# Hybrid decoder step: the last fixed expert pair added to the tokens by weighted slot matmuls

## The reference

```python
w_top = softmax(top_v) * p_sel                       # two weights per token
act = silu(hf @ w_eg[e]) * (hf @ w_eu[e])            # each expert: 1024 -> 256
out = out + (act * combine[:, e]) @ w_ed[e]          # 256 -> 1024
x = x + out
y = x * rsqrt(mean(x * x) + EPS) * norm_final
```

## Time and profile before

| | |
|---|---|
| Median of 3 runs | 797.81 us (797.54 to 798.9) |
| Profiled execution | 798.78 us, its span 796.7 us |
| Granted TensorE clock, mean | 0.979 |
| TensorE matmul, busy | 715.7 us, 90% |
| VectorE, ScalarE, GpSimd busy | 340.8, 246.0, 82.2 us |
| DMA | 172.49 MB, mean 216 GB/s |
| Chain that ended last | PE 69%, SP's queue 14%, DVE 8%, DMA 4%, ACT 3% |

### The profile page before, as it was taken

One profiled execution on the slowest core, in us unless ns is written; L12 is line 12 of the kernel. 1 busy time (PEld: TensorE's weight loads), 2 busy tenths in 40 slices (PEclk: granted clock), 3 DMA queues, 4 the chain that ended last, 5 costly groups with the idle time before them and its releaser, 6 DMA issues.

```text
span 796.7 us, 12378 instructions
## 1 busy us (share of the span) xinstructions
PE 715.7 (90%) x5118; PEld 534.2 (67%) x5118; DVE 340.8 (43%) x630; ACT 246.0 (31%) x496; POOL 82.2 (10%) x135
## 2 busy tenths in 40 slices
PE   4999999999999999999999999989999977777730
PEld 3888997778999999778999977864444422222210
DVE  6653359654565336435344532751323211111128
ACT  6233474544454342334222232411111100100013
POOL 2404000000000100000000010221113121111100
PEclk9999999999999999999999999989999999999985
DMA  8732111113132722613223289889999999999945
GB/s 314 230 107 62 54 53 53 54 53 106 54 98 62 264 82 99 220 53 97 62 80 110 78 297 398 302 284 374 419 415 418 418 418 417 419 419 419 412 163 219
DMA packets 82503, 172.49 MB, mean 216 GB/s; under 512 B 8064, under 2 KB 42208, under 8 KB 82432
## 3 DMA queue, kind: packets, MB, share of 16 engines
q1 hardware_dynamic: 72736, 148.51, 50.2%
q0 software_dynamic: 9712, 23.20, 7.9%
HBM read 162.73 MB, written 18.74 MB: 228 GB/s over the span
## 4 chain that ended last, share of the span: by engine, by line
PE 69%; SPq 14%; DVE 8%; DMA 4%; ACT 3%; issue 2%; POOLq 0%; ACTq 0%; DVEq 0%
PE bank L756 44%; SPq L566 10%; PE bank L1219 7%; PE bank L1235 4%; SPq L572 3%; DMA expert_down<-in_w_exp_down 2%; DVE w_split L1593 2%; PE bank L1151 1%; ACT w_split L1273 1%; PE bank L776 1%; PE bank L1186 1%; PE bank L1041 1%; PE bank L1047 1%; DMA x_rows<-in_x_prompt 1%; DVE token_out L2185 1%
## 5 line engine op out<-in xcount | busy, mean ns | idle before, releaser
L756 PE MATMUL bank<-hT_split,w_split 128*128 128x272 f32 x1152 | 154.1, 292 | 0.0
L756 PEld LDWEIGHTS bank<-hT_split,w_split 128*128 128x128 f32 x1152 | 147.4, 188 | 2.1 <-issue 0.9
L1219 PE MATMUL bank<-expert_gate_up,gatheredT 128*64 128x512 f32 x512 | 115.0, 595 | 21.3 <-DMA expert_gate_up<-in_w_exp_up 20.4
L756 PE MATMUL bank<-w_split,hT_split 128*128 128x512 f32 (+1 forms) x576 | 130.9, 381 | 0.4 <-DVE w_split L1593 0.4
L756 PEld LDWEIGHTS bank<-w_split,hT_split 128*128 128x128 f32 x576 | 100.6, 189 | 23.1 <-issue 3.3
L1593 DVE TENSOR_TENSOR w_split<-w_raw,w_split 128x2048 fp32r<-128x2048 f32 (+1 forms) x35 | 75.9, 2168 | 83.7 <-ACT w_split L1273 83.7
L1219 PEld LDWEIGHTS bank<-expert_gate_up,gatheredT 128*64 128x64 f32 x512 | 39.4, 137 | 93.7 <-issue 62.8
L1273 ACT ACTIVATE w_split<-w_raw 128x2048 fp32r<-128x2048 f32 (+1 forms) x35 | 63.4, 1812 | 42.4 <-PE bank L756 17.5
L1235 PE MATMUL bank<-expert_down,expert_actT 128*64 128x512 f32 x256 | 58.5, 597 | 13.2 <-DMA expert_down<-in_w_exp_down 8.1
L2156 DVE TENSOR_TENSOR expert_act<-expert_silu,bank 128x256 f32<-128x256 f32 x16 | 6.7, 421 | 119.5 <-ACT expert_silu L1547 119.5
L756 PE MATMUL bank<-gla_outT_split,w_split 128*128 128x272 f32 x384 | 49.4, 288 | 0.0
(11 more groups left out here) (372 smaller groups left out, 837.0 us busy)
## 6 DMA issues: line engine op xcount, KB each, us to landing
expert_gate_up<-in_w_exp_gate SPq DMA_DIRECT2D x64, 512.0 KB, 14.4
expert_gate_up<-in_w_exp_up SPq DMA_DIRECT2D x64, 512.0 KB, 15.3
expert_down<-in_w_exp_down SPq DMA_DIRECT2D x32, 1024.0 KB, 17.2
w_raw<-in_w_in SPq DMA_DIRECT2D x15, 1024.0 KB, 5.5
w_raw<-in_w_in SPq DMA_DIRECT2D x16, 512.0 KB, 4.7
s_state<-in_state_gla POOLq DMA_DIRECT2D x4, 1024.0 KB, 9.5
out_sample_gla_state<-s_state POOLq DMA_DIRECT2D x4, 1024.0 KB, 6.1
w_raw<-in_w_proj_gla SPq DMA_DIRECT2D x8, 512.0 KB, 4.4
```

What stands on the lines that cost most here:

```text
L756: ins = mm(out, stat(x, k), mov(y, k), start=first and n == 0 and m == 0, stop=last and n == len(ks) - 1 and m == 2)
L1219: ins = mm(P[2 + u][64 * half:64 * half + 64, :].rearrange("p (m n) -> p m n", m=2), XT[0][:, k, 64 * half:64 * half + 64], WGU[gb][:, k / ...
```

## The change

- Pair 15 (the last fixed pair, now always done last, outside the loop) isn't scattered. Its result stays in `YO`. A one-hot matrix, slot by token, carries each slot's weight (`SPREAD_LAST`), and a matmul adds the pair to the tokens in PSUM. The slots' weights come from ten small matmuls behind pair 1 (three bf16 digits).
- For blocks 0 to 2 the second expert's rows are added in PSUM too, by a matmul with a diagonal of `w2`. For the sampled block one matmul (`ST4`) makes `x + w1 * y1 + w2 * y2`.
- Rows of `tok_d` that pair 15 would have written must be zero, so GpSimd stores zeros to all 1088 rows in nine chunks, each behind one unit from 22 to 30.
- The rows are read back behind pair 14's scatter, to a weight buffer that pair 13 used last.
- The row `norm_final` is spread behind the tenth pair, and `keep_clock(5)` becomes `keep_clock(6)`.
- Two pairs are done after the loop (14 and 15), the loop does pairs 12 and 13 and any overflow, and the overflow pieces shift.

```diff
-PEELED = NFIX // 2 - 1
+PEELED = NFIX // 2 - 2
+SEQ = NFIX - 2
+ZERO_CHUNKS = -(-2 * NTOK // 128)
+BY_PE = (0, 1, 2)
...
+    YI = [at(f"token_out_{n}", [128, D], F, D0 + 49152 + 4096 * n) for n in range(2 * NB - 2)]
...
-            sp.wait_ge(scattered[0], 16 * turns)
-            sp.wait_ge(scattered[1], 16 * turns)
+            for kh in range(2):
+                sp.wait_ge(gu_done, 2 * (SEQ - 3) + kh + 1)
+                load_gate_up(2, pair(SEQ), kh)
+            sp.wait_ge(dn_done, SEQ - 2)
+            load_down(2, pair(SEQ))
...
+            sp.wait_ge(scattered[0], 16 * turns + 16)
             for bl in range(NB):
                 for k in range(2):
-                    sp.dma_start(YI[2 * bl + k][0:rows(bl), :],
-                                 tok_d[k * NTOK + bl * 128:k * NTOK + bl * 128 + rows(bl), :]).then_inc(x_in[bl], 16)
+                    dst = YI[2 * bl + k][:] if bl < 4 else X2[32 + 32 * k:64 + 32 * k, 4, :]
+                    sp.dma_start(dst, tok_d[k * NTOK + bl * 128:k * NTOK + bl * 128 + rows(bl), :]).then_inc(x_in[bl], 16)
...
+            pool.memset(ZEROS[:], 0.0).then_inc(pool_wrote, 1)
+            pool.wait_ge(pool_wrote, 1)
+            for c in range(ZERO_CHUNKS):
+                pool.wait_ge(main_mm, unit_done(OUT_UNIT - ZERO_CHUNKS + c))
+                n = min(128, 2 * NTOK - 128 * c)
+                pool.dma_start(tok_d[128 * c:128 * c + n, :].rearrange("p (c n) -> p c n", n=256),
+                               ZEROS[0:n, :].unsqueeze(1).to_broadcast([n, 4, 256])).then_inc(zeros_stored, 16)
...
-            pool.dma_start(NFIN[0:1, :], a["norm_final"].unsqueeze(0)).then_inc(nfin_in, 16)
...
+            pool.wait_ge(zeros_stored, 16 * ZERO_CHUNKS)
             for i in range(PEELED):
                 for u in range(2):
                     move_rows(i, u)
+                    if 2 * i + u == 2:
+                        pool.dma_start(NFIN[0:1, :], a["norm_final"].unsqueeze(0)).then_inc(nfin_in, 16)
+                        pool.wait_ge(slots_hot, 5)
+                        for k in range(2):
+                            pool.dma_start(W4[32 + 32 * k:64 + 32 * k, :], R1[f"w{k + 1}"][0:32, 4:5]).then_inc(w4_in, 16)
...
+            move_rows(turns, 0, last=True)
...
-            pe.wait_ge(nfin_in, 16)
-            for c in range(2):
-                ins = mm(P[2 + c][:], ONEROW[:], NFIN[0:1, 512 * c:512 * c + 512], start=True, stop=True)
-            ins.then_inc(nfin_mm, 1)
-            keep_clock(5)
+            keep_clock(6)
...
-                pe.wait_ge(gathered[v], 16 * i + (16 if u == 0 else 32))
-                turn_rows(v)
+                if not (last and u):
+                    pe.wait_ge(gathered[v], 16 * i + (16 if u == 0 else 32))
+                    turn_rows(v)
...
+                    if 2 * i + u == 1:
+                        pe.wait_ge(slots_hot, 5)
+                        slot_table(P[5][:, 320:323], OHR, LASTD, range(2 * NB)).then_inc(table_mm, 1)
...
+                    if 2 * i + u == 9:
+                        pe.wait_ge(memset_done, 2)
+                        pe.wait_ge(nfin_in, 16)
+                        for c in range(2):
+                            ins = mm(P[2 + c][:], ONEROW[:], NFIN[0:1, 512 * c:512 * c + 512], start=True, stop=True)
+                        ins.then_inc(nfin_mm, 1)
+                        pe.wait_ge(nfin_out, 1)
...
+            for u in range(2):
+                expert_pair(turns, u, last=True)
+
+            pe.wait_ge(spread_ready, 1)
+            for bl in range(NB):
+                cols = slice(128 * bl, 128 * bl + rows(bl))
+                banks = [P[2 * (bl % 4) + c][0:rows(bl), :] for c in range(2)]
+                if bl == 4:
+                    pe.wait_ge(x3_ready, 1)
+                if bl in BY_PE or bl == 4:
+                    pe.wait_ge(x_in[bl], 16 + 32)
+                    for c in range(2):
+                        half = slice(512 * c, 512 * c + 512)
+                        if bl == 4:
+                            mm(banks[c], ST4[0:96, :], X2[0:96, 4, half], start=True, stop=False)
+                        else:
+                            mm(banks[c], DIAG2[bl][:], YI[2 * bl + 1][:, half], start=True, stop=False)
+                if bl == 0:
+                    pe.wait_ge(y_out_a, 2 * turns + 3)
+                    pe.wait_ge(y_out_v, 2 * turns + 3)
+                for c in range(2):
+                    ins = mm(banks[c], SPREAD_LAST[:, cols], YO[:, 512 * c:512 * c + 512], start=bl not in BY_PE and bl < 4, stop=True)
+                ins.then_inc(sums_mm, 1)
...
+                    if j == 0:
+                        act.wait_ge(zeros_stored, 16 * ZERO_CHUNKS)
...
+                    if 2 * i + u == 9:
+                        act.wait_ge(nfin_mm, 1)
+                        A(NFIN[:, 0:512], P[2][:], ACT.Copy)
+                        A(NFIN[:, 512:D], P[3][:], ACT.Copy).then_inc(nfin_out, 1)
...
+                if bl < 4:
+                    act.wait_ge(x3_ready, bl + 1)
+                else:
+                    act.wait_ge(sums_mm, NB)
...
-            V.memset(ONEROW[:], 1.0)
...
+            V.tensor_tensor(SLOT[:, 0:1], IF1[:, NFIX - 1:NFIX], P[6][:, 2 * NFIX - 1:2 * NFIX], ALU.add)
...
+            for k in range(2):
+                js = slice(NB * k, NB * k + NB)
+                link(V.tensor_tensor(LASTW[:, js], R1[f"w{k + 1}"][:], PAIRH[:, js, NFIX - 1], ALU.mult))
...
+            V.tensor_copy(LASTD[:, :, 2, 0], LASTR[:]).then_inc(slots_hot, 1)
+
+            def last_weights():
+                dve.wait_ge(table_mm, 3)
+                V.tensor_reduce(SLOT[:, 1:2], P[5][:, 320:323], axis=AX.X, op=ALU.add)
+                V.memset(W4[0:32, :], 1.0)
+                V.memset(ONEROW[:], 1.0).then_inc(memset_done, 1)
...
-            OVER_PARTS = {1: over_tiles, 2: over_ranks, 3: over_places, 4: over_onehots, 5: over_experts, 6: over_turns, 9: over_rows}
+            OVER_PARTS = {3: last_weights, 1: over_tiles, 2: over_ranks, 4: over_places, 5: over_onehots, 6: over_experts, 7: over_turns, 9: over_rows}
...
+                if last and u:
+                    first_expert(0)
+                else:
+                    dve.wait_ge(xg_turned, n + 3)
+                    xt_half()
...
+            link(V.memset(IONES[:], 1.0))
+            link(V.tensor_tensor_scan(out=IOTA[:], data0=IONES[:], data1=IONES[:], initial=-1.0, op0=ALU.mult, op1=ALU.add))
+            V.scalar_tensor_tensor(out=SPREAD_LAST[:], in0=IOTA[:], scalar=SLOT[:, 0:1], in1=SLOT[:, 1:2].to_broadcast([128, NTOK]),
+                                   op0=ALU.is_equal, op1=ALU.mult)
+            for bl in BY_PE:
+                V.scalar_tensor_tensor(out=DIAG2[bl][:], in0=ident, scalar=R1["w2"][:, bl:bl + 1], in1=ident, op0=ALU.mult, op1=ALU.mult)
+            same = cst("same_head")
+            dve.wait_ge(w4_in, 32)
+            for p0, p1, q in ((0, 64, 0), (64, 96, 64)):
+                ins = V.scalar_tensor_tensor(out=ST4[p0:p1, :], in0=same[p0:p1, q:q + 32], scalar=W4[p0:p1, :],
+                                             in1=same[p0:p1, q:q + 32], op0=ALU.mult, op1=ALU.mult)
+            ins.then_inc(spread_ready, 1)
+            added = {}
+
+            def first_expert(bl):
+                y1 = YI[2 * bl][:]
                 dve.wait_ge(x_in[bl], 16 + 32)
-                link(V.scalar_tensor_tensor(out=y1[0:n, :], in0=y1[0:n, :], scalar=R1["w1"][0:n, bl:bl + 1], in1=X2[0:n, bl, :],
-                                            op0=ALU.mult, op1=ALU.add))
-                V.scalar_tensor_tensor(out=y1[0:n, :], in0=y2[0:n, :], scalar=R1["w2"][0:n, bl:bl + 1], in1=y1[0:n, :],
-                                       op0=ALU.mult, op1=ALU.add).then_inc(x3_ready, 1)
+                chain[0] += 1
+                added[bl] = chain[0]
+                V.scalar_tensor_tensor(out=y1, in0=y1, scalar=R1["w1"][:, bl:bl + 1], in1=X2[:, bl, :],
+                                       op0=ALU.mult, op1=ALU.add).then_inc(dve_step, 1)
+
+            def second_expert(bl):
+                y1 = YI[2 * bl][:]
+                dve.wait_ge(dve_step, added[bl])
+                chain[0] += 1
+                added[bl] = chain[0]
+                V.scalar_tensor_tensor(out=y1, in0=YI[2 * bl + 1][:], scalar=R1["w2"][:, bl:bl + 1], in1=y1,
+                                       op0=ALU.mult, op1=ALU.add).then_inc(dve_step, 1)
+
+            def banks_sum(bl):
+                y1 = two_halves(YI[2 * bl][:])
+                dve.wait_ge(dve_step, added[bl])
+                dve.wait_ge(sums_mm, bl + 1)
+                V.tensor_tensor(y1, BANKS[:, 2 * bl:2 * bl + 2, :], y1, ALU.add).then_inc(x3_ready, 1)
 
...
-            for bl in range(NB + 1):
-                if bl < NB:
-                    add_experts(bl)
-                if bl:
-                    last_norm(bl - 1)
+                x3, y = (YI[2 * bl][:], YI[2 * bl][:]) if bl < 4 else (None, OUT4[0:n, :])
```

(46 more changed lines are left out.)

83 lines of the change are left out of this document (55 added, 28 removed).

## The result

The changed kernel takes 788.74 us (median of 4 runs, 785.64 to 790.65) against 797.67 (797.09 to 798.90) for the kernel before on the same chip. The ratio is 0.9882, with a 95% interval of 0.9848 to 0.9916. The profiled execution has a span of 786.6 us, 10.1 less than before.

What follows compares the result with a forecast made beforehand. Matmuls were taken to bound the kernel up to about 535 us, then the stream of expert weights, then the tail. Span 796.7 - 9.1 - 0.5 = 787.1; time 788.2 us off the median, own range 787.0 to 789.5.

Steps and rivals of the forecast that it cites:

- Part 1: Tail: scatter and reads leave the path, first rows at 763.9; delay taken as 0, other bound 3.3 us.
- Part 2: Tail on TensorE: nine pairs of new-sum matmuls at 1.73 us, 15.6 us, ending at 780.6.
- Part 3: Tail on VectorE: 16.6 us of work, ending at 785.2 instead of 794.36; the tail gives back 9.1 us.
- Part 4: Before pair 0: norm matmuls leave, a sixth clock-keeping matmul comes; start up to 1.1 us earlier, 0.5 us saved.
- rival 1: Pair 0 meets the half clock: up to 6.0 us, 3.5 for half of its first half; chance 0.13.
- Part 5: Work costed at nothing: zeros in the projection units, slot weights, norm's 3 us stop behind pair 9, other small moves.
- Rival 2: Tail: reads delay the last weights (3.3 us, 791.5) or VectorE's half of the copy (2.2 us, 790.4); chance 0.12.
- Rival 3: Tail: the final sums run at half clock and the kernel is slower, 802.2 us; chance 0.04.

Runs made afterwards that it cites:

- late_reads: Changed kernel, with SP also waiting for pair 15's down matmuls before it reads the tokens back; 796.19 us, 0.9980 of the kernel before.
- block0_dve: Changed kernel, with TensorE making the second products of blocks 1, 2 and 3 instead of 0, 1 and 2, VectorE block 0's; 786.98 us, 0.9864.
- seconds_dve: Changed kernel, with the second products of blocks 0, 1 and 2 moved from TensorE to VectorE; 788.54 us, 0.9888.
- norm_back: Changed kernel, with the norm row spread ahead of pair 0 again, five clock-keeping matmuls and no stop behind pair 9; 788.72 us, 0.9877.
- zeros_three: Changed kernel, with each chunk of zeros stored three times, to the scratch and two spare ones nobody reads; 789.35 us, 0.9895.
- hold_more: Changed kernel, with 14 keep-clock calls instead of 6 ahead of the gathered rows and 2 more ahead of the last slot table; 787.81 us, 0.9878.
- after: The changed kernel itself, in its first measurement and profile, against the kernel before; 788.74 us, 0.9882.
- hold_clock: Changed kernel, with 10 keep-clock calls instead of 6 ahead of the gathered rows and 2 more ahead of the last slot table; 787.45 us, 0.9867.

## Why the prediction was right, and where it was not

The forecast was 788.2 us; it is 788.74, and the forecast's own range held it. The tail, 9.1 us of the 9.6, was foreseen with its mechanism. That the total came so near is in part luck: pair 0 started 3.3 us earlier where 1.1 was forecast, and the loss that the first rival named took that back.

**Part 1** held. Pair 14's scatter landed 6.9 us after 750.2, the reads were issued at 757.16, and the rows were there at 762.95, a microsecond sooner than the 763.9 taken (the weights were 0.9 sooner too); the order of the queue held too, as the last weights took 18.08 us and not longer than the 18.20 of the earlier trace rows. The bound of 0 was the right end, and late_reads confirms it (217.4 us from pair 0's end without reads under the weights, 217.0 with them). The Trainium skill says that each DMA engine consumes a queue's descriptors in ring order ("DMA: Bandwidth & Descriptors", Queues, rings and completion order); by that rule reads behind the weights in one queue don't delay them, and the trace agrees. late_reads shows what the part is worth: without the early reads 7.0 of the 9.2 us are gone, 1.9 of them by the clock.

**Part 2** held closely: a pair of matmuls took 1.72 us (1.73), and the slot pair of block 0 ended at 767.7 (768.5), 0.8 sooner because the weights had landed 0.9 sooner.

**Part 3** held: the last norm ended at 784.18 (785.2), again 0.9 of it from the earlier start, and a bank sum took 1.23 (1.25). The term was 9.1 us and measured 9.2. It was put down to VectorE alone, though; the chain binds on TensorE until 774.6. The prediction gave TensorE 1.7 us to spare, and it had none up to there. The two are so nearly even that the moves of work between them changed the tail by only 0.3 us less (block0_dve) and 1.0 us more (seconds_dve).

**Part 4** is the step that failed: "Pair 0 may start at 535.6 instead of 536.68, 1.1 us earlier if the clock is then as before", with 0.5 us taken from it. The rows landed in 4.98 us, not the 6.1 of the earlier trace rows, 0.9 us of the start is the execution's own, and pair 0 started 3.3 us earlier. With the clock as before that would have been worth 3 us: the matmuls would have ended at 540.5. But the clock fell, which cost 2.95 us in pair 0, and the term measured 0 in this profile, where 0.5 was forecast; norm_back agrees. That is rival 1, given 0.13, with a price near the 3.5 us it named for half of the matmuls; only the earlier rows paid for it. Where the clock fell early enough, in block0_dve, the term was 2.3 us. Its argument "against" came from another kind of row: a gap of 1.66 us in the stream lies between heavy matmuls; this one of 2.00 us lies ahead of small transposes and a second wait of 0.90. Which of these differences counts no run separates.

The reason given for Part 4's size was also off. I counted how much room the DMA engines had around pair 0 and took half of it. The runs show a plainer rule for this kernel: the stream's end stands 217.0 to 218.2 us behind the end of pair 0's matmuls. These free the first buffer, half by half. In the changed kernel's profile the DMA engines run dry and stand still from 540 to 541, after SP issues the first half of pair 3's loads at 540.06; it issues the second half at 543.49, 0.03 us behind pair 0's last matmul:

```profile
540.00:541.00 1.00, 1.00 (x8) 0.31 (x5) 0.00 (x0) 0.00 (x0) 0.00 (x0) 1.00 0.00 0
```

The rest runs at 417 GB/s (550 to 757). A microsecond at pair 0 is about a microsecond at the end. That the buffer is the reason is read from these rows; in block0_dve, where the engines don't run dry, part of the gain was lost.

**Part 5** held for the zeros (zeros_three) and for the rest in effect, but one of its numbers was half of what it should be. The norm's stop behind pair 9 was costed at 3 us of TensorE. The timeline and a window of the changed kernel:

```profile
666.85 1.98 PE L1307 MATMUL bank<-norm_final_rows,ones_row 1*128 1x512 f32 x4
670.00 10.02 PE L1273 MATMUL bank<-expert_gate_up,gatheredT 128*64 128x512 f32 x32 [1.17 <-ACT norm_final_rows L1650]
...
689.82 2.37 PE L1273 MATMUL bank<-expert_gate_up,gatheredT 128*64 128x512 f32 x10 [0.76 <-DMA expert_gate_up<-in_w_exp_up]
```

```profile
670.00:676.00 6.00, 6.00 (x16) 1.72 (x18) 0.00 (x0) 0.00 (x0) 1.03 (x1) 0.50 1.03 416
```

The stop is 3.15 us (666.85 to 670.00), and the clock falls in it, which adds 2.9 behind it (10.02 for 7.09). The DMA engines stay full meanwhile, and from 689.82 TensorE waits for weights again: the 6 us are covered. norm_back, without the stop, has 217.4 us from pair 0 to pair 15, no less than the 217.0 with it.

**Rival 2** did not occur. **Rival 3** did not occur in the changed kernel, whose last slice is at full clock, but late_reads shows its mechanism at work once TensorE is idle 5.02 us. The Trainium skill calls the throttled clock the default that activity releases ("TensorE: Matmul & The Clock Gate", Part 1); late_reads and pair 0 agree with that, and in the changed kernel the read rows come early enough for TensorE not to stop.

The account is then: 9.2 us from the tail, 0.9 of this one profile that begin in its first 21 us, 0 from pair 0. The medians of the changed kernel in three jobs lie 8.9, 9.2 and 9.3 us under those of before, the 9.2 of the tail. The forecast was 0.5 us too low, as much as Part 4's 0.5; but four executions that spread over 5 us can't show that the one is the other.

What stays open: why the clock falls in the keep-clock group in some executions and at pair 0 in others, and how often. Seven profiles of the same front part (five to two) and the spread of the times fit, but executions without a profile don't show it: their mean granted clock is on record (0.990 to 0.996 for the changed kernel's fourteen) and doesn't say where it fell. Whether hold_more's edit is worth its 1.3 us on the median is open for the same reason. That filling the whole wait keeps the clock rests on three profiles with it and seven without.

## To carry to other kernels

In this kernel, work that left the path ahead of the stream was worth only what the last engine before the stream gained *at its clock*: when a stretch is shortened so that TensorE comes to wait, price the matmuls behind the wait at both clocks. Find the one event from which a saturated stream runs to its end (here pair 0's last gate and up matmul) and measure changes against that, not against the room in the queues. And when a tail is handed from a DMA round trip to TensorE and VectorE, walk both engines' lists, as each is soon the bound of the other.

## What was not expected of the hardware

- The clock falls while TensorE works as well as behind a wait. In the profile of block0_dve TensorE is busy for all of 528 to 530 and granted 0.50; before that, up to 526.8, it had waited 0.25 and 0.94 us among small matmuls. In the profile of after the same waits stand at the same place, the same instructions ran at 1.00, and the fall came between 532 and 534, at pair 0.
- The length of the wait doesn't set the loss: 2.00 us of wait ahead of pair 0 cost 2.95 us (after), 3.18 us cost 1.7 (late_reads, 8.77 for 7.09); there the clock fell between 534 and 535 and was back at 538.
- A stop of 3.15 us with small work in it (four one-row matmuls and a wait of 1.17 us) brought the clock down behind pair 9 in the midst of the stream, and cost about as much again (2.9 us).
- The same gather landed in 6.1 us before and in 4.98 us in the changed kernel; why is not settled. It is no effect of the change alone: hold_clock had 6.1, late_reads 6.16, norm_back 4.7.
